# Four of sixteen cache pages per sequence asked for by ScalarE instead of SyncE

## What is computed

```python
ckv_all = concatenate([cache_ckv[l][page_table].reshape(DB, past_len, KV_RANK), ckv], axis=1)
kpe_all = concatenate([cache_kpe[l][page_table].reshape(DB, past_len, QK_ROPE), kpe], axis=1)
s = einsum('bqhc,bkc->bhqk', q_lat, ckv) + einsum('bqhr,bkr->bhqk', q_rope, kpe)
p = softmax(where(k_pos <= q_pos, s * SM_SCALE, -inf))
o_lat = einsum('bhqk,bkc->bqhc', p, ckv)
```

## Time and profile before

| | us |
|---|---|
| median of 3 runs | 1967.04 |
| lowest and highest of the 3 | 1962.96, 1975.54 |
| the profiled execution's own time | 1964.54 |
| its span, first to last instruction | 1962.8 |
| the stage with the sample sequences, roughly | 385 to 545 |

### The profile page before, as it was taken

One profiled execution on the slowest core, in us unless ns is written; L12 is line 12 of the kernel. 1 busy time (PEld: TensorE's weight loads), 2 busy tenths in 40 slices (PEclk: granted clock), 3 DMA queues, 4 the chain that ended last, 5 costly groups with the idle time before them and its releaser, 6 DMA issues.

```text
span 1962.8 us, 26325 instructions
## 1 busy us (share of the span) xinstructions
PE 1794.8 (91%) x8673; PEld 1360.8 (69%) x8673; DVE 1509.3 (77%) x3499; ACT 628.3 (32%) x1094; POOL 611.8 (31%) x454
## 2 busy tenths in 40 slices
PE   7998899888798996999787899999999999999995
PEld 3656583344467634667576668888888888888883
DVE  5025348677837638899987779999899999999987
ACT  1322121322211201114446334343433343443333
POOL 0000001077620135210000124555455555556630
PEclk9998899867765597999899999999999999999997
DMA  7521324299842367544346898999999999999981
GB/s 283 195 89 43 118 114 167 72 329 341 311 152 90 106 243 264 229 156 146 134 186 253 313 323 331 378 398 373 368 408 403 370 388 387 398 386 388 387 301 45
DMA packets 159766, 508.68 MB, mean 259 GB/s; under 512 B 15248, under 2 KB 76224, under 8 KB 138176
## 3 DMA queue, kind: packets, MB, share of 16 engines
q1 hardware_dynamic: 95168, 272.73, 37.7%
q0 software_dynamic: 64512, 234.91, 31.9%
HBM read 474.69 MB, written 31.45 MB: 258 GB/s over the span
## 4 chain that ended last, share of the span: by engine, by line
PE 36%; DVE 35%; issue 10%; DMA 10%; ACT 3%; SPq 3%; POOL 1%; DVEq 1%; ACTq 0%
PE ps L1105 5%; DVE lo L2179 5%; PE ps L1089 4%; PE ps L688 4%; PE ps L1035 4%; DMA lo<-eu 4%; DVE ul L2148 3%; PE ps L1051 2%; PE ps L1076 2%; PE ps L997 2%; DVE lo L1752 2%; DMA lo<-vr,lo 2%; SPq L519 2%; PE ps L797 2%; DVE hi L2179 1%
## 5 line engine op out<-in xcount | busy, mean ns | idle before, releaser
L1609 POOL DMA_INDIRECT lo<-ur,lo x224 | 310.0, 1384 | 797.1 <-DVE lo L2115 323.6
L1609 POOL DMA_INDIRECT lo<-vr,lo x224 | 298.2, 1331 | 482.0 <-DVE lo L2187 300.2
L1105 PE MATMUL ps<-vh,hx 128*128 128x512 f32 x768 | 242.4, 397 | 22.4 <-DVE vl L2152 17.9
L1089 PE MATMUL ps<-xh,uh 128*128 128x320 f32 x832 | 257.8, 310 | 0.0
L1089 PE MATMUL ps<-xl,uh 128*128 128x320 f32 x832 | 257.1, 309 | 0.0
L1089 PE MATMUL ps<-xh,ul 128*128 128x320 f32 x832 | 256.8, 309 | 0.0
L1211 ACT ACTIVATE hi<-ps 128x512 f32<-128x512 f32 (+11 forms) x251 | 146.5, 627 | 317.5 <-PE ps L1035 108.4
L1105 PE MATMUL ps<-vl,hx 128*128 128x512 f32 (+1 forms) x768 | 240.3, 394 | 0.0
L2179 DVE SCALAR_TENSOR_TENSOR lo<-lo 128x1024 f32<-128x1024 f32 x168 | 215.1, 1280 | 15.8 <-DMA lo<-vr,lo 4.8
L1105 PEld LDWEIGHTS ps<-vh,hx 128*128 128x128 f32 x768 | 139.8, 190 | 59.1 <-issue 31.3
L2152 DVE TENSOR_TENSOR vl<-hi,vh 128x1024 fp32r<-128x1024 f32 x128 | 156.1, 1219 | 21.2 <-ACT vh L1211 12.6
(11 more groups left out here) (413 smaller groups left out, 2876.1 us busy)
## 6 DMA issues: line engine op xcount, KB each, us to landing
hi<-ev SPq DMA_DIRECT2D x64, 1024.0 KB
hi<-wts SPq DMA_DIRECT2D x22, 2048.0 KB, 7.9
hi<-eu SPq DMA_DIRECT2D x38, 1024.0 KB, 5.8
lo<-eu SPq DMA_DIRECT2D x26, 1024.0 KB
gates<-hi SPq DMA_DIRECT2D x10, 2048.0 KB, 8.1
hi<-gates SPq DMA_DIRECT2D x30, 640.0 KB
lo<-cache SPq DMA_DIRECT2D x64, 144.0 KB
hi<-cache SPq DMA_DIRECT2D x64, 144.0 KB
```

The lines of the kernel that those rows point to most:

```text
L1089: last = nc.tensor.matmul(ps[:, 6 + p, 0:GW[1]], a[p][:, k * 128:(k + 1) * 128], b[:, k, :], start=(k == 0 and b is xh and a is uh), stop= ...
L1105: last = nc.tensor.matmul(ps[m, 2 * slot(i) + half, :], a, b[p][:, half * 512:(half + 1) * 512], start=(first and n == 0), stop=(final and ...
L1609: nc.gpsimd.indirect_dma_start(ring[n % RING], None, table, bass.IndirectOffsetOnAxis(idxs[:, i, k:k + 1], 0)).then_inc(r_in[n % RING], 16)
```

## The change

A constant `SP_PAGES = 12`. For the sequences b = 2 to 7, SP reads 12 row numbers and asks for pages 0 to 11. ACT reads the other four row numbers of sequence b + 1 and asks for pages 12 to 15, on the even turn of sequence b, between `mla_pt(j - 2)` and `sm_exp(b)`; before the transfers it waits for `sm_o >= b`, the same event that SP waits for with its part of sequence b + 1. All 16 transfers still add to the same semaphore, and the waits for the pages are as before. The sequences 0 and 1 stay wholly with SP.

```diff
+SP_PAGES = 12
@@ SP's list
             def page_rows(b):
                 return [sp.value_load(pfirst[0:1, b * PAGES + k:b * PAGES + k + 1], min_val=0, max_val=cache.shape[0] - PAGE)
-                        for k in range(PAGES)]
+                        for k in range(PAGES if b < 2 else SP_PAGES)]
@@ ACT's list
+            def page_rows(b):
+                return [act.value_load(pfirst[0:1, b * PAGES + k:b * PAGES + k + 1], min_val=0, max_val=cache.shape[0] - PAGE)
+                        for k in range(SP_PAGES, PAGES)]
+
+            def load_pages(b, rows):
+                for k, row in zip(range(SP_PAGES, PAGES), rows):
+                    nc.scalar.dma_start(cach[b % 2][:, k, :], cache[bass.ds(row, PAGE), :]).then_inc(c_in[b % 2], 16)
@@ attention, after mla_exp(j), mla_pt(j - 2)
                     if samples and b < SB:
+                        if not odd and 1 <= b < SB - 1:
+                            rows = page_rows(b + 1)
+                            act.wait_ge(s["sm_o"], b)
+                            load_pages(b + 1, rows)
                         if odd:
                             sm_factor(b)
                             if b + 1 < SB:
                                 sm_near(b + 1)
                         else:
                             sm_exp(b)
```

## The result

The changed kernel takes 1979.73 us (median of 9 runs, 1971.2 to 1983.85). The kernel before, run beside it, takes 1970.07 us (9 runs, 1962.96 to 1975.54). The ratio is 1.0049, with a 95% interval of 1.0029 to 1.0070: slower by 9.7 us, 5.7 to 13.8 by the interval. The time lies in the predicted range, but the forecast was no change, and this is a loss clear of noise. The prediction took 1%, 20 us, as the least that a measurement of this kernel can tell; the interval here is about 4 us to either side. The profiled execution had 1979.73 us with a span of 1977.9. The trace of before is of an execution 5.5 us under that kernel's median, so the two traces differ by 15.1 us of span where the medians differ by 9.7; what they differ by is in the right place, but somewhat too large.

The account below looks back on a forecast made before the run. A loop over two sequences through SP's loads was taken to set the pace: gaps gained 5.2 us, late sm_exp lost 5.3, sum +0.1. Trace 1964.6 us, plus 2.5 to the median, gave 1967 us; range 1957 to 1982.

Parts of the forecast that it names:

- the gaps between sm_o and SP's start: SP's loads start after sm_o is there; six gaps, 9.2 us in all, 5.2 us gained on the loop through 3, 5, 7.
- The price on ACT: Four row numbers and four transfers on ACT before sm_exp, taken at SP's price: 4.3 us a sequence.
- ACT itself waits for the pages 37.9 us in seven times afterwards: On ACT after sm_exp: its page waits, 5.4 us each, absorb every delay in ACT's own list.
- The prediction's own delays of sm_exp: On ACT, sequences 1 to 6: sm_exp later by ACT's price less the idle before it, 12.5 us in all.
- over two sequences through SP: Pace-setting loop: load starts, pages land, sm_near to sm_o, load of the sequence after next; gains 5.2, loses 5.3, sum +0.1 us.
- The slower one: Rival: ACT's four pages land last and make a loop over one sequence; 1971 to 1984 us, chance 0.19.
- the 7.3 us from which it was to decide: Time from ACT's last issue to landing above which late pages set the pace: 18.93 - 11.6 us; 6.5 taken.
- The rival of the gained gaps: Rival: gaps before SP's loads are gained and ACT's delay is not lost; 1961.5 us, 1958 with all gaps; chance 0.15.
- Double price: Rival: ACT's instructions before sm_exp cost 8.6 us instead of 4.3; 1980 or 1988 us, chance 0.05.
- SP's wait for L866: Sign on SP: a wait for sm_o should appear about five times, 3 to 5 us each.
- The idle before L1317: Sign on ACT: its idle before sm_exp, waiting for DVE's least, should vanish.
- The rule of the Trainium skill that was weighed: Issuing engines share the same 16 transfer engines; several save only initiation time; by it alone, gain at most 5.2 us.

Follow-up runs that it names:

- e2: Kernel before, with SP asking for 16 pages at fixed places from sequence 2 on, without row numbers, nothing added on ACT: 1966.18 us, ratio 0.9998.
- e1: Kernel before, with eight unused row-number reads on ACT before sm_exp and no transfers there: 1975.81 us, ratio 1.0041.
- e5: Kernel before, with sixteen row-number reads on ACT before sm_exp and no transfers there: 1991.78 us, ratio 1.0127.
- e3: The change with ACT's four row numbers and four transfers moved earlier, between mla_exp(j) and mla_pt(j - 2): 1965.31 us, ratio 0.9999 to the kernel before.
- e4: The change with ACT's four row numbers and four transfers moved behind sm_exp(b): 1965.57 us, ratio 0.9990 to the kernel before.
- e9: The change with SP_PAGES = 8, so ACT asks for eight pages before sm_exp: 2000.87 us, ratio 1.0166 to the kernel before.
- e7: Kernel before with e6's moved dot product and e4's page split together: 1968.57 us, ratio 0.9991.
- e6: Kernel before, with one of three even-turn dot products on DVE moved from before sm_least to behind sm_least and sm_out: 1969.39 us, ratio 1.0006.
- e12: Kernel before with 6 instead of 8 gathers a sequence (the rest run in the stage behind), e4's page split and e6's moved dot product: 1958.35 us, ratio 0.9947.

## Why the prediction was wrong

**What bounds the stage.** Right that SP's large part of the chain was no measure of its worth: e2 shows 0, within some 5 us. Wrong in the rest: the gaps between sm_o and SP's start were counted as a gain. In the trace with SP relieved SP no longer works through them (it waits 62.8 us), and they bring nothing; what grew there was DVE's wait for gathered rows, 13.6 us in place of 8.8.

**The price on ACT.** Right: 4.3 us were taken; in sequence 3 the four reads and four issues took 3.9 (455.45 to 457.41 for the reads, 1.91 for the issues), and 3.5 to 4.4 in the others from 2 on. Only the first time was dearer, 7.6 us. The 7.60 us of idle before sm_exp of sequence 2 are 4.4 us of this price and then DVE's late least.

**The step that failed: "ACT itself waits for the pages 37.9 us in seven times afterwards, 5.4 each, so ACT's own list absorbs every delay."** A wait of ACT is a reserve for ACT alone. What depends on sm_exp goes through PE, to the next sequence's L833, and there the idle was 1.68, 0.28, 0.63, 0, 0 and 4.77 us. It also goes through DVE and POOL to the gathered rows and the next least, where the sequences 2 to 4 had none. The prediction's own delays of sm_exp, 2.1, 4.3, 1.0, 0, 2.2 and 2.9 us, less these give 0.4 + 4.0 + 0.4 + 0 + 2.2 + 0 = 7.0 us. With the first transfer's extra 3.3 us it is 10.3, and 9.7 were measured. This estimate was made afterwards, and that it comes so near is in part luck: it leaves out the way through DVE and takes ACT's idle before sm_exp as a fixed cover, while the least itself moved with the sm_exp before it. So the mistake was not in the size of a term but in the choice of the loop: over two sequences through SP, with gaps as gain and +0.1 us as the sum, where the one that bound was over one sequence. That the place before sm_exp is what costs is shown: reads alone there lose 8.1 us (e1) and 25 us (e5), the same four pages at two other places lose nothing (e3, e4).

**The rivals.** The slower one had the right sign, 1971 to 1984, for the wrong reason. ACT's pages did land late: all 16 were there 5.5 to 9.3 us after ACT's last issue (435.83 to 445.09 for sequence 3), in four of six sequences beyond the 7.3 us from which it was to decide; 6.5 were taken. It did not decide, since PE was later still. e1 has the loss without one transfer on ACT. The rival of the gained gaps is out, since e2 has no gain. Double price is out by the rows above; the same loop prices it, as e9 with twice the instructions lost 33 us.

**The signs named.** SP's wait for L866 in five times, SP gone from the chain, the loads within 0.3 us of L866's end: right. The size of that wait, 3 to 5 us each: wrong, 7.4. The idle before L1317 was to vanish: wrong, it grew from 2.4 to 4.8 us on average over the sequences 2 to 6. The share at 0.97 to 1.03: wrong, 0.88. sm_near of 7 at 515 to 520: wrong, 530.27, which is over the 6 us that were to show the prediction wrong. The wait of ACT for pages "from 5.4 to some 3 to 5 us": 2.5 us. The rule of the Trainium skill that was weighed (DMA: Bandwidth & Descriptors, Issuing engines are not separate DMA queues) agrees with what was measured: issuing from a second engine can save only the time to initiate, and with the issues out of the way (e3, e4) the ratios are 0.9999 and 0.9990.

**Left open.** PE's granted clock was 0.62 of full speed from 405 to 530 us, with PE busy for 84% of the time; before it was 0.71 with 88% from 405 to 517. At the lower of its two levels L834 took 1.12 us, at the higher 0.66. What part of the loop's length is this and not the wait itself, no run separates; nor how much of the wait for gathered rows the second queue adds. Nor is it settled what binds e7.

## What to carry to other kernels

A wait in an engine's list is a reserve for that engine's own next instruction only. To price a delay, follow its product to every engine that uses it and read that one's idle before the instruction that needs it; here these were PE and DVE. When the profile shows full transfers and a loop of the same length, relieving one may give nothing: here neither alone (e2, e6) nor both (e7) gave anything that can be measured, and only with fewer gathers beside them did the relief show (e12, 10 us). Put transfer issues where their engine is idle anyway (e3) or behind the instruction that others wait for (e4), not straight before it.

## What the hardware showed that was not expected

The first transfer that ACT asks for took 3.61 us to issue, against 0.34 us for the others. It was so in seven of the eight kernels with transfers on ACT (2.8 to 5.0 us; the exception is e9, where none took over 1.1 us). The timeline of ACT's queue after:

```profile
412.73 3.61 ACTq L1312 DMA_DIRECT2D lo<-cache  x1
```

And the twelve issues of that line with the one buffer; shortest, median and longest in ns:

```profile
L1312 ACTq DMA_DIRECT2D lo<-cache x12: 163/342/3612, 412.7 to 503.1; - x12
```

Here it cost some 3 us once: in sequence 1 DVE's least was there at 414.62, and sm_exp started at 417.90. Whether a transfer issued on ACT earlier would take it off the path was not tried.
